# Two transformer blocks on one core: state-space tables moved into the selected attention, a shorter routing, and another head and tail

## The reference, cut to what matters

```python
def token_mixer(h, ...):
    q, kv, nsa_g, u, merge_g = split(h @ w_in)
    attn = nsa_attention(q, kv, sigmoid(nsa_g))      # compressed + selected + window branch
    ssm = s5_mixer(u, ...)                           # diagonal complex state space, 32 groups x 64 states
    return (g_attn * (attn @ nsa_w_o) + g_ssm * (ssm @ ssm_w_o)) @ w_out

def hier_moe(h, ...):                                # 32 experts in 4 groups, 2 per token
    g_p, g_idx = top_k(softmax(h @ w_group + b_group), 1)
    e_p, e_idx = top_k(softmax(e_logits of that group), 2)
    w = g_p * e_p / sum(e_p)
    ...                                              # tokens sorted by expert, padded to blocks
    return sum over both experts of w * ((silu(x @ w_gate[e]) * (x @ w_up[e])) @ w_down[e])

x = x + g1 * token_mixer(...);  x = x + g2 * hier_moe(...);  out = rms_norm(x, final_g)
```

## Time and profile before

| | |
|---|---|
| median of 3 runs | 1857.25 us (1855.82 to 1861.77) |
| profiled execution | 1857.5 us, its span 1856.2 us |
| TensorE busy | 1680.1 us (91%) |
| VectorE busy | 941.0 us (51%) |
| ScalarE busy | 720.5 us (39%) |
| GpSimd busy | 244.6 us (13%) |
| mean granted clock of TensorE | 0.952 of full |
| moved from HBM | 293.99 MB, 169 GB/s over the span |

### The profile page before, as it was taken

One profiled execution on the slowest core, in us unless ns is written; L12 is line 12 of the kernel. 1 busy time (PEld: TensorE's weight loads), 2 busy tenths in 40 slices (PEclk: granted clock), 3 DMA queues, 4 the chain that ended last, 5 costly groups with the idle time before them and its releaser, 6 DMA issues. The chain is left out here.

```text
span 1856.2 us, 23943 instructions
## 1 busy us (share of the span) xinstructions
PE 1680.1 (91%) x9050; PEld 1260.8 (68%) x9050; DVE 941.0 (51%) x1851; ACT 720.5 (39%) x1604; POOL 244.6 (13%) x225
## 2 busy tenths in 40 slices
PE   6999969978999999979998699999999939999991
PEld 4887759967888888867877477877888823333330
DVE  4752464545666676664427766643336661222215
ACT  3432762235333334453323566664334521212211
POOL 0000016001222220000000011110010112333320
PEclk9999979989999999989999799999999959999996
DMA  6321000042344442422300000006222348999953
GB/s 255 116 91 46 1 1 1 1 182 90 152 186 185 185 182 96 183 91 105 123 0 24 4 5 8 8 8 249 91 91 91 137 180 350 401 374 387 391 201 152
DMA packets 40080, 251.66 MB, mean 136 GB/s; under 512 B 17760, under 2 KB 17888, under 8 KB 23456
## 3 DMA queue, kind: packets, MB, share of 16 engines
q1 hardware_dynamic: 23120, 223.49, 30.8%
q10 hardware_dynamic: 3024, 15.07, 2.1%
q0 software_dynamic: 13824, 11.58, 1.9%
HBM read 293.99 MB, written 18.87 MB: 169 GB/s over the span
## 5 line engine op out<-in xcount | busy, mean ns | idle before, releaser
L600 ACT ACTIVATE units<-arena 128x512 fp32r<-128x512 f32 (+1 forms) x434 | 261.2, 626 | 487.2 <-PE banks L2206 483.1
L1185 DVE TENSOR_TENSOR units<-arena,units 128x512 fp32r<-128x512 f32 x388 | 263.8, 704 | 290.6 <-ACT units L600 290.3
L2204 PE MATMUL banks<-hx,units 128*128 128x512 f32 x800 | 315.2, 394 | 2.8 <-DVE arena L1633 1.7
L2205 PE MATMUL banks<-hx,units 128*128 128x512 f32 x800 | 312.3, 390 | 0.0
L2206 PE MATMUL banks<-hx,units 128*128 128x512 f32 x800 | 312.3, 390 | 0.0
L600 ACT ACTIVATE arena<-banks 128x512 f32<-128x512 f32 (+3 forms) x238 | 135.0, 571 | 267.9 <-PE banks L2141 101.8
L2141 PE MATMUL banks<-arena 128*128 128x128 f32 (+3 forms) x700 | 116.6, 301 | 67.3 <-ACT arena L600 17.7
L2204 PEld LDWEIGHTS banks<-hx,units 128*128 128x128 f32 x800 | 151.0, 189 | 34.4 <-issue 3.4
L2206 PEld LDWEIGHTS banks<-hx,units 128*128 128x128 f32 x800 | 150.8, 189 | 31.8
L2205 PEld LDWEIGHTS banks<-hx,units 128*128 128x128 f32 x800 | 151.0, 189 | 30.8
L2204 PE MATMUL banks<-units 128*128 128x512 f32 x416 | 164.3, 395 | 6.1 <-DVE units L1185 6.0
(11 more groups left out here) (409 smaller groups left out, 2411.9 us busy)
## 6 DMA issues: line engine op xcount, KB each, us to landing
arena<-in_moe_gu SPq DMA_DIRECT2D x32, 2048.0 KB
arena<-in_w_in SPq DMA_DIRECT2D x17, 2048.0 KB
arena<-in_moe_dn SPq DMA_DIRECT2D x32, 1024.0 KB, 9.1
arena<-in_ada SPq DMA_DIRECT2D x12, 2048.0 KB
arena<-in_w_gu SPq DMA_DIRECT2D x11, 2048.0 KB
arena<-in_w_out SPq DMA_DIRECT2D x4, 2048.0 KB
arena<-in_w_down SPq DMA_DIRECT2D x4, 2048.0 KB
arena<-in_cmp_w SPq DMA_DIRECT2D x2, 2048.0 KB
```

The costliest lines, as they stand in the source:

```text
L600: return func(dst, src, ACT.Copy, scale=scale)
L1185: tt(U[:, u % 4, 1, :], src, U[:, u % 4, 0, :].bitcast(F32), SUB).then_inc(*up("gemm_dve", "lo", c.part, u))
L2204: pe.matmul(bs[i], sh[:, q], mh, start=c.first and k == 0, stop=False)
L2205: pe.matmul(bs[i], sh[:, q], ml, start=False, stop=False)
```

## The change

- Head: `cols` 0 to 79 (`ln1` and the convolution weights) are loaded by themselves, right behind the identity; the rest goes ahead of the remaining constants. SP waits for `w_in0` before it loads `w_in1`.
- State space: `ssm_rot(1..3)`, `ssm_tables` and ScalarE's `ssm_turns` go into the first `LEAD = 12` turns of the selected attention; `ssm` starts after them on all engines. Their scratch moves into the area of constants that are no longer read. `ssm_tables` yields six times.
- Routing: operations over all four tiles at once; `first_max` with five operations instead of six; the exponential's users and the table of extra blocks stand elsewhere in the order; places with three matmuls instead of fourteen, from running sums; `ohi` is waited for in two parts.
- Tail: the gain `g2` is multiplied in at `rows_out`, which VectorE now does for both halves. A tile of the tail takes two operations. The root's table is loaded ahead. The product of tile 0 is split: VectorE multiplies by `fg` before the root is known, ScalarE by the root.

```diff
@@ layout and scratch @@
+        o = CONST_AT["triU"][0]
+        self.mag = self.cst[:, o:o + 288].rearrange("p (l g) -> p l g", l=9)
...
+LEAD = 12
@@ act_program @@
     def ssm():
+        for i in range(LEAD):
+            yield
+            if i == 7:
+                ssm_turns()
         for f in range(4):
...
     a.dma_start(m.cst[:, 0:256], I["consts"][:, 0:256]).then_inc(*up("dma_id", by=16))
+    a.dma_start(m.col[:, 0:80], I["cols"][:, 0:80]).then_inc(*up("dma_ln", by=16))
...
-        if t == 0:
-            a.dma_start(m.col, I["cols"]).then_inc(*up("dma_col", by=16))
     root("ln1", m.r4, m.rs_tmp[:, 0:4])
-    a.wait_ge(*at("dma_col"))
+    a.wait_ge(*at("dma_ln"))
...
     first_gemm("w_in0", "ln1", m.x0, m.x0, m.r4, hx_hi, 0)
+    a.dma_start(m.col[:, 80:], I["cols"][:, 80:]).then_inc(*up("dma_col", by=16))
     a.dma_start(m.cst[:, 256:], I["consts"][:, 256:]).then_inc(*up("dma_cst", by=16))
...
     cmp_pt(3)
-    ssm_turns()
     fence(15)
...
-        rows_out("dn", i, out_of(i))
-        if i % 2 == 0 and i:
-            rows_out("dnd", d - 1, more_of(d - 1))
     more_hidden(NPAIR // 2 - 1)
-    rows_out("dnd", NPAIR // 2 - 1, NBLK - 1)
-
+
+    func(m.rs_tmp[:, 63:64], ones1, ACT.Sqrt)
...
     root("fg", m.r4, m.rs_tmp[:, 0:4])
+    a.wait_ge(*at("norm_dve", "rstd", "fg"))
+    a.wait_ge(*at("fin_dve", "fg"))
+    copy(m.x4[:, 0, :], m.x4[:, 0, :], m.r4[:, 0:1]).then_inc(*up("fin_act", "out", 0))
@@ dve_program @@
     def ssm():
 
         ch = Chain(v, s, "ssm_dve")
+        for f in range(1, 4):
+            yield
+            yield
+            ssm_rot(f)
+        yield from ssm_tables()
         v.wait_ge(*at("dma_ssm"))
...
     for t in range(4):
-        if t < 3:
-            ssm_rot(t + 1)
         cmp_sums(t)
         if t < 2:
             cmp_scores(t + 2)
         cmp_out(t)
-    ssm_tables()
     fence(15)
...
     def rows_out(key, i, n):
-        v.wait_ge(*at("moe_pe", key, i, 1))
-        if n >= 4:
-            v.wait_ge(*at(f"yo{n % 4}", n - 4))
-        v.tensor_copy(m.yo[n % 4][:, 512:1024], s.bank("moe", key, i, 1)).then_inc(*up("moe_dve", "yo", n))
+
+        for half in range(2):
+            q = slice(512 * half, 512 * half + 512)
+            v.wait_ge(*at("moe_pe", key, i, half))
+            if n >= 4 and half == 0:
+                v.wait_ge(*at(f"yo{n % 4}", n - 4))
+            tt(m.yo[n % 4][:, q], s.bank("moe", key, i, half), m.grow[:, q], MUL).then_inc(*up("moe_dve", "yo", n, half))
...
         ch(stt(y1, y2, R(4)[:, t:t + 1], y1, MUL, ADD))
-        ch(stt(y1, y1, R(5)[:, t:t + 1], m.grow, MUL, MUL))
-        ch(tt(m.x4[:, t, :], m.x4[:, t, :], y1, ADD), "x", t)
+        ch(stt(m.x4[:, t, :], y1, R(5)[:, t:t + 1], m.x4[:, t, :], MUL, ADD), "x", t)
+    v.wait_ge(*at("dma_fg"))
+    v.wait_ge(*at("norm_act", "sq", "fg", 0))
+    ch(tt(m.x4[:, 0, :], m.x4[:, 0, :], m.fg, MUL), "fg")
     v.wait_ge(*at("norm_act", "sq", "fg", 3))
     rstd("fg", m.r4, m.ss, 1024.0)
-    v.wait_ge(*at("dma_fg"))
-    for t in range(4):
+    for t in range(1, 4):
...
@@ dve_route @@
-        ch(ts(tmp_, onehot, -64.0, 64.0, MUL, ADD))
-        ch(tt(tmp_, tmp_, io, ADD))
+        ch(stt(tmp_, onehot, -64.0, io, MUL, ADD))
...
-    for t in range(4):
-        ch(tt(t3[:, t], lg[:, t, 4:36].rearrange("p (g e) -> p g e", g=4), bc(go[:, t, :].unsqueeze(2), 4, 8), MUL))
-        ch(v.tensor_reduce(el[:, t, :], t3[:, t].rearrange("p g e -> p e g"), AX, ADD))
+    ch(tt(t3, lg[:, :, 4:36].rearrange("p t (g e) -> p t g e", g=4), bc(go.unsqueeze(3), 4, 4, 8), MUL))
+    ch(v.tensor_reduce(el, t3.rearrange("p t g e -> p t e g"), AX, ADD))
...
+    for k in range(2):
+        ch(tt(mk2[:, k].rearrange("p t (g e) -> p t g e", g=4), bc(go.unsqueeze(3), 4, 4, 8),
+              bc(oh[k].unsqueeze(2), 4, 4, 8), MUL))
+    ch(tt(mks[:, 0, :], fl2(mk2[:, 0]), fl2(mk2[:, 1]), ADD), "mks")
+    for t in range(1, 4):
+        ch(tt(mks[:, t, 0:32], mks[:, t - 1, 0:32], mks[:, 0, 32 * t:32 * t + 32], ADD), "sums", t)
+
+    v.wait_ge(*at("route_act", "gexp"))
+    ch(v.reduce_sum(R(1), ge, AX))
...
+    ch(tt(m.both, bc(bp.rearrange("p a t n -> p a (t n)").unsqueeze(2), 2, 2, 128),
+          bc(mk2.rearrange("p k t n -> p k (t n)").unsqueeze(1), 2, 2, 128), MUL))
+    ch(v.tensor_reduce(m.bi, m.both.rearrange("p a k (t n) -> p (a k t) n", t=4), AX, ADD))
...
@@ pool_program, pe_program, sp_program @@
-        g.wait_ge(*at("moe_act", "yo", n))
-        g.wait_ge(*at("moe_dve", "yo", n))
+        g.wait_ge(*at("moe_dve", "yo", n, 1))
...
+        for _ in range(LEAD):
+            yield
...
-    for t in range(4):
-        group(b[:, 32 * t:32 * t + 32], [(K["triS"], m.mks[:, t, :])] + [(ones, m.mks[:, u, :]) for u in range(t)])
-    group(b[:, 128:160], [(ones, m.mks[:, t, :]) for t in range(4)]).then_inc(*up("route_pe", "pos"))
+    pe.matmul(b[:, 0:128], K["triS"], m.mks[:, 0, :], start=True, stop=False)
+    pe.wait_ge(*at("route", "sums", 3))
+    pe.matmul(b[:, 32:128].rearrange("p (t n) -> p t n", t=3), ones, m.mks[:, 0:3, 0:32], start=False, stop=False)
+    pe.matmul(b[:, 128:160], ones, m.mks[:, 3, 0:32], start=False, stop=True).then_inc(*up("route_pe", "pos"))
...
         load(name)
+        if name == "w_in0":
+            sp.wait_ge(*at("ring0", "w_in0"))
```

More of the change, by code:

```diff
@@ L388, in moe_views @@
         self.go, self.ge = new(4, 4), new(4, 4)
-        self.mk2 = [new(4, 32) for _ in range(2)]
-        self.mks, self.pos, self.q_, self.blk = new(4, 32), new(4, 32), new(4, 32), new(4, 32)
-        self.cnt, self.nov, self.cum, self.ob = new(32), new(32), new(32), new(32)
-        self.bk, self.ik, self.hk = new(2, 4), new(2, 4), new(2, 4)
-        self.ohi, self.ohb = new(4, 256), new(8, 2 * NBLK)
+        o_dd = self.top
+        four = lambda a: new(a, 128).rearrange("p a (t n) -> p a t n", t=4)
+        self.mk2, self.bp = four(2), four(2)
+        self.mks, self.q_ = new(4, 128), new(4, 32)
+        self.both = self.mks.rearrange("p (a k) n -> p a k n", a=2)
+        self.nov, self.cum, self.ob = new(32), new(32), new(32)
+        self.bi, self.hk = new(16), new(2, 4)
+        self.ohi = new(8, 128).rearrange("p (k t) n -> p k t n", k=2)
+        self.ohe, self.ohb = new(8, NBLK), new(8, 2 * NBLK)
         self.tb_, self.td_ = new(2, NBLK), new(2, NBLK)
-        self.dd = new(2, NDYN, 32)
+        self.dd = self.at(o_dd, 2, NDYN, 32)
         self.ej, self.full = new(NDYN), new(NDYN)
@@ L1914, in dve_route @@
     ch(tt(R(4), R(3), R(2), SUB), "esub")
+    mk2, mks, q_, bp = m.mk2, m.mks, m.q_, m.bp
+    nov, cum, ob, hk = m.nov, m.cum, m.ob, m.hk
+    blk, pos = bp[:, 0], bp[:, 1]
+    bk, ik = m.bi[:, 0:8].rearrange("p (k t) -> p k t", k=2), m.bi[:, 8:16].rearrange("p (k t) -> p k t", k=2)
+    for k in range(2):
[6 more added lines that the diff above has]
+    ch(v.reduce_sum(R(1), ge, AX))
+    ch(v.reciprocal(R(1), R(1)))
     v.wait_ge(*at("route_act", "eexp"))
@@ L1918, in dve_route @@
     ch(tt(R(5), R(5), R(1), MUL))
[L1919 to L1925 removed]
     b = s.bank("route", "pos")
+    places = b[:, 0:128].rearrange("p (t n) -> p t n", t=4)
     v.wait_ge(*at("route_pe", "pos"))
[L1928 to L1933 removed]
+    ch(ts(nov, b[:, 128:160], 1.0 / 64, -32.5 / 64, MUL, ADD))
     ch(ts(nov, nov, RND, RND, ADD, SUB))
@@ L2642, in down @@
         for n in range(2):
-            b = take(("moe", key, i, n), (("moe_act", "moe_dve")[n], "yo", n_out))
+            b = take(("moe", key, i, n), ("moe_dve", "yo", n_out, n))
             for k in range(2):
```

98 lines of the change are left out of this document (39 added, 59 removed).

## The result

The changed kernel takes 1830.74 us (median of 4 runs, 1829.67 to 1831.51), the kernel before on the same chip 1859.08 us (4 runs, the three of the table above and one more). The ratio is 0.9848, with a 95% interval from 0.9829 to 0.9867: 28 us faster, between 25 and 32. The forecast was 1832.9, made as 24.6 us off 1857.5. The profiled execution has a span of 1828.4 us where it was 1856.2, so 27.8 us less.

A forecast was written before the change was run, and what follows sets the result against it. TensorE, busy 1680.1 of 1856.2 us, was taken as the bound, so only its standstills could be won: 4.9 + 15 - 11.5 + 10.1 + 0 + 6.1 = 24.6 us off 1857.5, giving 1832.9; range 1827 to 1841.5.

The forecast's parts named there:

- Head, 4.9: Start of the kernel: the small `cols` load lets TensorE's first transposes start near 12.85 instead of 17.74; 4.9 us gained.
- Compressed attention, 15: Before the selected attention: rotations and tables leave VectorE, and eight matmuls may keep the full clock; 15 us gained.
- Selected attention, 11.5 back: Twelve lead turns: VectorE's moved rotations and tables set their pace, so 11.5 us are lost again.
- Routing, 10.1: Routing up to the gathers: fewer, larger VectorE operations and fewer TensorE records make indices ready sooner; 10.1 us gained.
- Expert loop, 0: Expert loop: eviction halves moving from ScalarE to VectorE fit into its idle time; no change, bounds -2 and 1.
- Tail, 6.1: After the last scatter: tiles at 2.6 us instead of 3.90 and an earlier table load; 6.1 us gained.
- The 5 us for the low clock: First group of the selected attention: the 5 us it lost to the low clock before needn't be lost again.
- The 8 us of TensorE's work in the lead: Lead turns: TensorE's useful work there, some 8 us, subtracted from a lead of 22 to give a cost of 14.
- the lead costs as much as it frees: Rival on the lead turns: 16 us back instead of 11.5, with 13 out, giving 1839.5; chance 0.2.
- The lead is cheap: Rival on the lead turns: TensorE keeps 2.4 GHz, 16.5 us out and 6 back, giving 1825.8; chance 0.14.
- The slow rival: TensorE's clock falls in the lead and stays at 0.50 in the selected attention; over 0.3% slower; chance 0.02.
- The 14 us back: Selected attention: with the full price of a clock restart it gives back 14 us instead of 11.5; total 1835.4.

The follow-up runs named there:

- two rotations early: Changed kernel with two moved rotations put back into idle VectorE stretches of the compressed attention; 1841.65 us with 7 lead turns, 1828.26 us with 8.
- The empty lead: Changed kernel with rotations, tables and sines back ahead of fence 15, but twelve turns of attention alone before the state-space work; 1837.98 us (0.9878).
- tables beside the dense projection: Changed kernel with tables made in VectorE's gaps beside the dense projection, rotations in idle stretches of the compressed attention, no lead turns; 1818.48 us (0.9772).
- tables back: Changed kernel with the three rotations, the tables and ScalarE's sines back ahead of fence 15 and no lead turns; 1840.44 us (0.9893).
- the indices before the block table: Changed kernel with the routing's token table and indices placed ahead of the block table, as in the kernel before; 1827.34 us (0.9823).
- the extra matmuls: Changed kernel with one more, unused matmul of 128 x 512 in each of the twelve lead turns; 1835.22 us (0.9876).

## Why the prediction was right, and where it was off

The time lay 2.2 us below the forecast of 1832.9 and well inside the range; the second set of runs of the changed kernel had 1832.30. In the profiles the gain was 27.8 us where the sum had 24.6. By its own steps:

- **Head, 4.9.** Right where it was made (4.6: x landed 0.25 us later and so the scalings). Its step "4.9 us" was carried to the end of the sum unchanged, and 1.6 us of it were lost where the full clock came later in the work: 1.05 already in the first matmuls of `w_in0`, the rest by 840 us. `kcT` stood at 988.3 to 990.0 in thirteen profiles with this head, 992.6 in the one before: the gain is 2.6 to 4.3.
- **Compressed attention, 15.** It was 16.3. "With 2.6 us of idle left they may stay at 2.4 GHz and take 1.9 us" came true to the number (2.56 and 1.97), and the clock stayed full until the first score. The 14.6 us of VectorE's work and the 1.8 us of these matmuls make 16.4; the choice of 15 was what missed. The free first rotation was free; "two rotations early" shows that a second can be too, ahead of the copy of `kcT`. The idle time left before the first score was 2.26 us, where under 2 was forecast.
- **Selected attention, 11.5 back.** It was 10.5, and the mechanism is the one named: VectorE's queue sets the lead, up to the end of the tables at 22.3 us (22.9 forecast). The empty lead puts the price of the table work at 9.3. But the nearness of the number is partly luck, since steps inside were off against each other. "TensorE reaches turn 12 after 21 to 23 us": it was 26.0, at the very mark of "a lead over 26 us" that was to show the prediction wrong, since TensorE ran the lead at half clock and waited 1.8 us for ScalarE behind the sines. That ScalarE's block of 6.3 us would cost nothing was one part that fell; how much of the 4 us is the clock's stays open. Against it the clock was full again as the state space began, so the 2.5 us kept for that were not paid. With both put right the working gives 26.0 - 8 - 5 = 13.0 and not 10.5, so another term was off by 2.5 us. The 5 us for the low clock would have to be larger, and the runs speak against that: "tables beside the dense projection", which had 0.50 only at the start of the stage instead of for 10 us, gained 3.0 us on "tables back". The 8 us of TensorE's work in the lead were too few: it was busy for 17.7 of the 26.0 us at a mean clock of 0.54, which makes some 9.6 us at full clock, an estimate. The last us stays open.
- **Routing, 10.1.** 10.7, with `mks` and the three sums after 6.3 us (6.3 forecast), positions after 7.5 (7.5), the first token matmul after 15.1 (14.9), indices after 22.3 (22.3). The reserve of 0.4 us for gathers that meet the down loads wasn't needed here; "the indices before the block table" shows that the meeting is real 2.6 us earlier. The mechanism is the one named, and nearly every step of it came to the number.
- **Expert loop, 0.** The profile had 2.8 us less, but the same kernel's loop then took 297.8 us, and eleven other profiles 292.6 to 298.4. Neither of the two parts of the change that touch the loop moved it out of that spread. 2.8 of the 3.2 us by which the profile was better than the sum are this luck; the misses of the other terms nearly cancel (-1.9, +1.3, +1.0, +0.6, -0.4, and -0.2 where nothing was forecast).
- **Tail, 6.1.** 5.7: the tiles gave 4.6 instead of 5.0, because the y rows of tile 1 came 3.1 us behind those of tile 0 and not 2.5, so VectorE waited 0.50 us; the table load gave its 1.0.

The rival *the lead costs as much as it frees* is out: in "tables back" the two stages together take 6 us more than in the changed kernel. (The sum of this rival comes to 1839.4, not 1839.5, and that of the next to 1825.9, not 1825.8.) *The lead is cheap* was half right: 16.3 out, but 10.5 back, not 6, and TensorE did not keep 2.4 GHz in the lead. The slow rival's mechanism, a clock that stays at 0.50 in the selected attention, was not seen in any profile. The Trainium skill (TensorE: Matmul & The Clock Gate, "What's actually happening") has the low state as the default, released by activity. The trace agrees: 0.50 in the thin lead, 1.00 for most of it with the extra matmuls. The 14 us back that the prediction set beside it were not borne out: the measured 10.5 decides.

## What to carry to other kernels

- Work taken off one wait and put into a pipeline is paid there if the engine that does it becomes the one that sets the pace. Here 16 us were freed and 10 came back, because VectorE had the same work in its queue. Look first for a stage in which that engine is idle: the same operations beside a projection with VectorE half idle cost nothing that could be seen and gave 12 us more.
- When two periodic programs are interleaved, the shift of one against the other matters. One turn of shift, half a period of the scores, cost 13 us here.
- Before explaining 3 us in a stage, run the same kernel twice.

## What the runs showed of the hardware that I had not expected

The granted clock makes equal work unequal. Between the last T and the routing none of the experiments changes anything, and the stage takes 230.7 to 231.1 us in eight profiles and 232.5 to 234.4 in six. Windows over it, of the changed kernel:

```profile
1246.60:1477.40 230.80, 226.85 (x1035) 186.19 (x1036) 114.56 (x179) 98.21 (x173) 15.23 (x11) 0.99 0.35 133
```

and of the kernel with the tables back, with the same 1035 records of TensorE but 3.2 us more busy time, at 0.97:

```profile
1252.60:1486.30 233.70, 230.07 (x1035) 188.99 (x1036) 114.50 (x178) 98.18 (x173) 15.26 (x11) 0.97 0.35 131
```

The first 15 us of these windows have a granted clock of 0.77 in the changed kernel and of 0.54 with the tables back. So a kernel whose edit lies elsewhere can win or lose 3 us here, and what brings one or the other stays open.
